# First norm of a two-block model: square sums added by VectorE, token sums in single columns

## The reference

```
def rmsnorm(x, w):
    xf = x.astype(jnp.float32)
    y = xf * lax.rsqrt(jnp.mean(xf * xf, axis=-1, keepdims=True) + NORM_EPS)
    return (y * w.astype(jnp.float32)).astype(x.dtype)

u = rmsnorm(h, norm_w[i])
proj = jnp.einsum('bsd,de->bse', u, w_in[i])
```

## Time and profile before

| | us |
|---|---|
| median of three runs | 3244.74 |
| lowest, highest | 3243.88, 3247.97 |
| span of the profiled execution, its own time | 3236.3 |
| PE busy | 3109.7 (96%) |
| DVE busy | 1999.7 (62%) |
| ACT busy | 1299.9 (40%) |
| first norm, start to first projection | 31.6 |

### The profile page before, as it was taken

How to read it: one execution, slowest core, us unless ns; L and a number is a source line. 1 busy time by engine, 2 the same in 40 slices (tenths; PEclk the granted TensorE clock), 3 DMA queues, 4 the chain that set the end, 5 groups by cost and what they waited for, 6 DMA issues and landing times.

```text
span 3236.3 us, 47842 instructions
## 1 busy us (share of the span) xinstructions
PE 3109.7 (96%) x18134; PEld 2578.9 (80%) x18134; DVE 1999.7 (62%) x3834; ACT 1299.9 (40%) x2340; POOL 759.8 (23%) x324
## 2 busy tenths in 40 slices
PE   9999999999999989999899999999899999999987
PEld 6888888777777767877799889888677778777765
DVE  5676677555565657975755555556755555655555
ACT  5534443444444440022444444440344444454412
POOL 3223332322222213543211121113112112111221
PEclk9999999999999999999999999999999999999999
DMA  3111111111111137521200010153201111100141
GB/s 118 46 40 46 46 59 46 60 59 53 53 53 53 64 146 298 220 79 52 91 30 30 31 43 30 46 203 130 78 21 51 45 51 45 51 32 33 67 161 76
DMA packets 64828, 237.79 MB, mean 73 GB/s; under 512 B 7008, under 2 KB 10080, under 8 KB 63600
## 3 DMA queue, kind: packets, MB, share of 16 engines
q1 hardware_dynamic: 31680, 115.91, 9.9%
q10 hardware_dynamic: 32944, 119.10, 9.7%
HBM read 185.11 MB, written 49.87 MB: 73 GB/s over the span
## 4 chain that ended last, share of the span: by engine, by line
PE 79%; DVE 9%; ACT 5%; issue 2%; DVEq 2%; DMA 1%; ACTq 1%; SPq 0%
PE ps L1304 21%; PE ps L189 13%; PE ps L360 9%; PE ps L2223 7%; PE ps L1368 5%; PE ps L1334 4%; PE ps L1350 4%; PE ps L891 3%; PE ps L482 3%; PE ps L868 2%; PE ps L133 2%; DVE fox_l L1455 1%; PE ps L852 1%; DVE wa_l L941 1%; PE ps L853 1%
## 5 line engine op out<-in xcount | busy, mean ns | idle before, releaser
L210 POOL TENSOR_TENSOR w_hi<-raw,small 128x1024 fp32r<-128x1024 f32 x160 | 334.9, 2093 | 2393.7 <-PE ps L1304 1099.3
L212 POOL TENSOR_TENSOR w_lo<-raw,w_hi 128x1024 fp32r<-128x1024 f32 x160 | 424.8, 2655 | 22.8
L1304 PE MATMUL ps<-nb_u_hi,w_hi 128*128 128x512 f32 (+1 forms) x640 | 249.2, 389 | 6.1 <-DVE nb_q_lo L2470 4.2
L1304 PE MATMUL ps<-nb_u_hi,w_lo 128*128 128x512 f32 (+1 forms) x640 | 246.6, 385 | 0.0
L1304 PE MATMUL ps<-nb_u_lo,w_hi 128*128 128x512 f32 (+1 forms) x640 | 245.7, 384 | 0.0
L1466 DVE TENSOR_TENSOR nb_pt_lo<-ps,nb_pt_hi 128x512 fp32r<-128x512 f32 x208 | 143.9, 692 | 144.2 <-ACT nb_pt_hi L1393 143.9
L360 PE MATMUL ps<-u_hi,w_hi 128*128 128x512 f32 x528 | 212.8, 403 | 5.9 <-ACT silu_h L539 2.6
L1304 PE MATMUL ps<-u_hi,w_lo 128*128 128x512 f32 x512 | 208.9, 408 | 0.0
L360 PE MATMUL ps<-u_hi,w_lo 128*128 128x512 f32 x528 | 208.6, 395 | 0.0
L360 PE MATMUL ps<-u_lo,w_hi 128*128 128x512 f32 x528 | 208.4, 395 | 0.0
L1304 PE MATMUL ps<-u_hi,w_hi 128*128 128x512 f32 x512 | 208.3, 407 | 0.0
(11 more groups left out here) (357 smaller groups left out, 8027.8 us busy)
## 6 DMA issues: line engine op xcount, KB each, us to landing
raw<-in_w_stream SPq DMA_DIRECT2D x160, 512.0 KB, 3.3
h_sb<-in_w_ada ACTq DMA_DIRECT2D x16, 1024.0 KB, 5.0
nf_b<-nf_rows ACTq DMA_DIRECT2D x16, 512.0 KB, 4.4
nb_bias<-in_rel_bias ACTq DMA_DIRECT2D x16, 448.0 KB, 3.8
y_parts<-wa_y_hi ACTq DMA_DIRECT2D x8, 640.0 KB, 3.0
y_parts<-wa_y_lo ACTq DMA_DIRECT2D x8, 640.0 KB, 4.2
la_out_yh<-y_parts SPq DMA_DIRECT2D x8, 640.0 KB, 10.0
la_out_yl<-y_parts SPq DMA_DIRECT2D x8, 640.0 KB, 11.1
```

Of the source, the lines that this page charges most:

```text
L210: pool.tensor_tensor(w_hi[:, s, :], raw[:, s, :], zero, ALU.add)
L212: pool.tensor_tensor(w_lo[:, s, :], raw[:, s, :], w_hi[:, s, :].bitcast(F32), ALU.subtract).then_inc(w_ready, 1)
L1304: mm = pe.matmul(ps[:, b:b + ch["n"]], w(slot, k), u[:, k, ch["c0"]:ch["c0"] + ch["n"]], start=k == 0 and p == 0, stop=k == KT - 1 and p == 2)
```

## The change

ACT squares tile 0 into a new buffer `sum1`; tiles 1 to 6 go to the two old buffers in turn and tile 7 to a third one. DVE adds the squares of tiles 1 to 5 to `sum1` (five additions of 128 x 1024). TensorE takes the token sums three times, of `sum1`, of tile 6 and of tile 7, with `token_means`, all into one bank; ACT takes the root from this bank. The padding at the start grows from 16 to 60 matmuls. DVE's eight diagonal passes go, and a later norm's count of `stat_var` is one lower.

```
-        sq1 = sb("sq1", [P, 2, T], at=ph1)
+        sq1 = sb("sq1", [P, 3, T], at=ph1)
+        sum1 = sb("sum1", [P, T], at=ph1)
...
-                if k >= 2:
-                    act.wait_ge(n1_sum, k - 1)
-                nc.scalar.activation(sq1[:, k % 2, :], x_sb[:, k, :], ACT.Square).then_inc(n1_sq, 1)
+                if 3 <= k < KT - 1:
+                    act.wait_ge(n1_sum, k - 2)
+                nc.scalar.activation(sum1[:] if k == 0 else sq1[:, 2 if k == KT - 1 else k % 2, :], x_sb[:, k, :],
+                                     ACT.Square).then_inc(n1_sq, 1)
...
-            act.wait_ge(stat_var, 1)
-            standard_deviations(act, T, None, small[:, 1:2])
+            act.wait_ge(n1_mean, 1)
+            standard_deviations(act, T, 2, small[:, 1:2])
...
-            keep_busy(pe, 0, 16)
-            for k in range(KT):
+            keep_busy(pe, 0, 60)
+            pe.wait_ge(n1_sum, KT - 3)
+            token_means(pe, sum1, T, 2, 0, 3)
+            for k in range(KT - 2, KT):
                 pe.wait_ge(n1_sq, k + 1)
-                broadcast_means(pe, sq1[:, k % 2, :], T, 2, k == 0, k == KT - 1).then_inc(n1_sum, 1)
+                mm = token_means(pe, sq1[:, 0 if k == KT - 2 else 2, :], T, 2, k - (KT - 3), 3)
+            mm.then_inc(n1_mean, 1)
             spread_rows(pe, T, diag1, 6, 1, 16)
...
+            for k in range(1, KT - 2):
+                dve.wait_ge(n1_sq, k + 1)
+                dve.drain()
+                dve.tensor_tensor(sum1[:], sum1[:], sq1[:, k % 2, :], ALU.add).then_inc(n1_sum, 1)
             dve.wait_ge(loaded, 32)
-            dve.wait_ge(n1_sum, KT)
-            token_variances(dve, T, 2, diag1)
             inverse_diagonals(dve, T, diag1, 1)
```

More of the change, by code:

```diff
@@ L233, in build_program @@
         n1_sum = sem("n1_sum")
+        n1_mean = sem("n1_mean")
         n1_scaled = sem("n1_scaled")
@@ L2036, in act @@
                 load_sqrt_table(act)
-                act.wait_ge(stat_var, 2 + self.l)
+                act.wait_ge(stat_var, 1 + self.l)
                 standard_deviations(act, self.cols, None, small[:, 2:3])
```

## The result

The changed kernel took **3251.23 us** (median of 10 runs, 3248.91 to 3255.53), the kernel before 3243.34 us (10 runs, 3240.22 to 3247.97): a ratio of **1.0025** with a 95% interval of 1.0016 to 1.0034, so 7.9 us or 0.25% slower. The time lies in the predicted range and 2.7 us above the predicted value; the forecast of a difference within 0.2% fell just short, as most of the interval lies on the slower side of that bound.

The account below looks back on a forecast made before the run. A long train of TensorE matmuls was taken as the bound, the norm costing the time until the first projection. Span 3236.3 + 3.8 = 3240.1, plus 8.4 to the median, gave 3248.5 us; range 3242.5 to 3253.0.

Parts of the forecast that it names:

- the forecast of a difference within 0.2%: Whole time: change under 6.5 us, about what a measurement can tell; slower was given 0.15, faster 0.05.
- TensorE's queue holds the norm: First norm: padding delays the token sums to 17.4 us, whatever ACT and DVE gain; at unchanged clock spreading starts +0.6 us.
- The clock falls in the sums: One-column token sums: clock drops to 0.50 at 20.6 us, sums end at 24.8; +2.2 to +5.5 us, chance 0.47.
- Case E: Token sums: clock falls but they keep 0.113 us each, only padding pays; +2.7 us, 3247.4 us, chance 0.10.
- the middle stretch: Low clock from the sums into the second padding: lasts 6.7 us, back at 27.4, spreading at 29.6; +3.8 us.
- The long stretch: Low clock from the sums on: lasts 10 us, spreading matmuls start at 31.4 us; +5.5 us.
- Nothing behind the norm moves: After the first projection: everything waits for what came before, so a shift there moves the rest as one block.
- last sign of being wrong altogether: Whole kernel: prediction fails if the time moves by more than the first projection's start does.
- The sum's +3.8: Later start of the spreading matmuls, added to the profiled span: 3236.3 + 3.8 = 3240.1 us.
- case C: Clock falls in the sums and stays at 0.50 past the norm, over 10 us; +9.0 us, 3253.7 us, chance 0.11.
- The median is 8.4 above the span: Whole time: the runs' median lay 8.4 us above the profiled span, carried over from 3240.1 to 3248.5 us.

Follow-up runs that it names:

- the wide sums: The changed kernel with 64 equal columns instead of one in each token-sum matmul; 3246.87 us, 1.0018 of the kernel before.
- the short first padding: The changed kernel with a first padding of 16 matmuls instead of 60; 3252.62 us, 1.003 of the kernel before.
- the shift: The kernel before with a second padding of 40 matmuls instead of 16, for a later first projection; 3251.23 us, 1.0025 of the kernel before.
- 24 more: The kernel before with 24 more padding matmuls: 4 each in the first norm's second and third padding, 16 in the later norm's; 3247.61 us, 1.0016.
- the trimmed kernel: The changed kernel with 64-column sums, first padding 47 instead of 60 and second 9 instead of 16; 3245.17 us, 1.0007 of the kernel before.
- the pairs: The changed kernel with 64-column sums, DVE adding in pairs, a buffer per square, paddings of 40 and 9; 3246.91 us, 1.001 of the kernel before.
- 8 more: The kernel before with second padding 20 instead of 16 and third 16 instead of 12 matmuls; 3242.95 us, 1.0001 of the kernel before.
- 16 less: The kernel before with second padding 8 instead of 16 and third 4 instead of 12 matmuls; 3245.46 us, 1.0008 of the kernel before.

## Why the prediction was right, and where it was off

**TensorE's queue holds the norm: right.** First one-column matmul forecast at 17.4, seen at 17.35; no idle time of TensorE before the spreading. Squares (by 15) and additions (by 14.2) ended at 15.42 and 14.63, 0.4 us late each, under a cover of 2 us. That 17.4 fits to 0.05 us is luck: it was worked out from a first padding of 6.56 us, and with the same 120 records ahead of them the sums started at 16.55 in the changed kernel without the second padding.

**The clock falls in the sums: right**, at 20.6 by forecast and between 20.4 and 20.5 by the stretches; sums over at 24.8 by forecast, 24.6 seen. The moment is an estimate that came out well: in the changed kernel without the second padding the clock fell 2.2 us into the sums and not 3.1. Case E, in which weight loads keep their pace, would have ended them at 22.8 and is refuted: some 20 records from the fall to 24.61 took (24.61 − 20.45) / 20 = 0.21 us each, and their weight loads 0.33 us instead of the 0.19 before it. The Trainium skill (TensorE: Matmul & The Clock Gate, section LDWEIGHTS (loading the stationary operand)) gives a load's time by its columns alone, with no term for the clock; here it differs between the two levels, and the measurement decides.

**How long it stays low: mis-sized.** I took the middle stretch of the earlier trace rows, 6.7 us, on the reason that unbroken padding brings the clock back; the padding began at 24.61 and the clock was back only after 30.6, some 10.2 us after its fall. The long stretch, which I kept as the upper bound (+5.5, spreading at 31.4), is what happened: spreading at 31.17. Against the mean of the three profiles before (31.10) the first projection came 5.75 us later, where the sum had 3.8.

**Nothing behind the norm moves: wrong.** I wrote that a shift there moves the rest as one block, and left only 0.05 for what moves behind it, on the faster side. Its last sign of being wrong altogether was a time that moves by more than the first projection's start does, and it came true: 7.9 us against 5.2 (5.75 by the mean). The third piece grew from a mean of 9.75 to 12.02 us. So 5.75 + 2.27, less 0.3 in the last piece, gives 7.7 of the measured 7.9 us. The same sum gives 2.7 for the wide sums (3.3 measured), 8.7 for the short first padding (9.0), 7.0 for the shift (7.6), 4.6 for 24 more (4.3) and 1.7 for the trimmed kernel (2.2); it is off by 1.2 for the pairs (4.4 against 3.2), 1.7 for no second padding (5.1 against 6.8), 2.2 for 8 more (−2.2 against 0.0) and 2.4 for 16 less (0.1 against 2.5). The sum takes the second piece as equal everywhere, though it differs by 6 us between profiles of one kernel, so its closer fits are in part chance.

**The time inside the range: partly luck.** The sum's +3.8 is half of the measured 7.9 us. The top of the range was drawn for case C, a clock that stays low past the norm; the clock was back before the projection, and the rest of the time came from a place that the prediction put at nothing.

**"The median is 8.4 above the span": not a property of the kernel.** Each run lies 1.8 us above its span; the profiled execution before was about 5 us quicker than the median of its kernel (3243.34 − 1.8 − 3236.3). Adding the difference to the median was harmless, but that offset says nothing of the work around the span.

## What to carry to other kernels

Taking work off TensorE saves nothing while its queue holds padding of the same length, and work that replaces wide matmuls with very narrow ones must be priced with the clock that followed such a train elsewhere in the trace, at the longest low stretch as readily as at the middle one. Before a shift at the start is carried to the end, look for a place where two DMA queues race behind the same store: which of them goes first can turn on less than a microsecond, and cost a few. Controls that change only padding far from the place in question show whether it moves without the edit: of the three here one had the long wait.

## What the runs showed of the hardware

- 48 matmuls at one pace of about 0.113 us, each with its own weight load: with one column the granted clock went from 1.00 to 0.50 after 3 us (2.2 us in the changed kernel without the second padding), with 64 it was 1.00 over all 5.2 us. With 64 columns but idle times of 1.18 and 0.93 us around the first sums it fell too, at 17.8.
- At 0.50 a one-column matmul with its load takes (24.61 − 14.35) / 48 = 0.214 us, nearly twice as long; the 128-column weight load takes 0.33 us instead of 0.19.
- A DVE pass of 1.23 us took 2.28 and 3.29 us when it started inside a POOL pass; a POOL pass of 2.35 us that started inside a DVE pass took 3.15.
- Sixteen matmuls of padding in a norm at 1520 us and eight at the start moved a wait at 3110 us from 2.1–3.7 to 6.6 us, and the whole time by 4.3 us (2.3 to 8.1 by the ratio's interval).
- In the same kernel the later norm's padding ran up to its sums, without the 2.67 us of idle time of the earlier trace rows, and the clock did not fall behind them: the 12 matmuls of padding took 1.58 us instead of 2.88.
